# Attention scores of the second block: q's high part stacked over k's high and low parts, in one-pass matmuls

## The reference

```python
def chunked_rel_attention(q, k, v, rel_bias):
    ...
    s = jnp.einsum('bcqhd,bckhd->bhcqk', qc, kb).astype(jnp.float32) * (hd ** -0.5) + bias[None, :, None]
    ...
    s = jnp.where(valid[None, None, :, None, :], s, jnp.finfo(jnp.float32).min)
    p = jax.nn.softmax(s, axis=-1).astype(v.dtype)
    o = jnp.einsum('bhcqk,bckhd->bcqhd', p, vb)

def hybrid_mixer(x, mix_norm, w_in, ...):
    h = rms_norm(x, mix_norm)
    proj = h @ w_in
    ...
    xbc = jax.nn.silu(causal_depthwise_conv(xbc, conv_w, conv_b))
    y = ssd_chunked(xs, dt, a, bm, cm, d_skip).reshape(bsz, seqlen, SSD_INNER)
    y = rms_norm(y * jax.nn.silu(z.astype(jnp.float32)), ssd_norm).astype(x.dtype)
    att = chunked_rel_attention(...)
    return jnp.concatenate([y, att], axis=-1) @ w_out
```

## Time and profile before

| | |
|---|---|
| three runs, median (lowest to highest) | 2024.4 us (2022.7 to 2024.58) |
| the profiled execution, its own time | 2024.56 us |
| its span in the trace | 2022.8 us |
| PE busy | 1943.0 us, 96% |
| DVE, ACT, POOL busy | 972.6, 837.1, 791.6 us |
| the loop over the pairs | about 1344 to 1579 us, one pair 59.7 us |
| records of the score matmuls (line 814) | 64, 25.7 us busy |

### The profile page before, as it was taken

How to read it: one execution, slowest core, us unless ns; L and a number is a source line. 1 busy time by engine, 2 the same in 40 slices (tenths; PEclk the granted TensorE clock), 3 DMA queues, 4 the chain that set the end, 5 groups by cost and what they waited for, 6 DMA issues and landing times.

```text
span 2022.8 us, 25020 instructions
## 1 busy us (share of the span) xinstructions
PE 1943.0 (96%) x8654; PEld 1559.7 (77%) x8654; DVE 972.6 (48%) x1099; ACT 837.1 (41%) x1072; POOL 791.6 (39%) x353
## 2 busy tenths in 40 slices
PE   2999999998999999999999999999998999999998
PEld 1777777776788888888888888777676788888886
DVE  6666666666534333223344331447786634344323
ACT  2566666663455554223232222355555323232221
POOL 4222222224344444444444444432222344444443
PEclk9999999999899999999999999899999999999999
DMA  6233333331222222222222233222111222222321
GB/s 274 103 126 124 124 123 126 124 125 69 75 94 97 95 94 102 94 102 85 99 98 93 95 104 107 79 84 73 67 68 54 73 93 94 97 100 93 104 104 73
DMA packets 54324, 202.59 MB, mean 100 GB/s; under 512 B 6032, under 2 KB 6160, under 8 KB 53392
## 3 DMA queue, kind: packets, MB, share of 16 engines
q1 hardware_dynamic: 54288, 202.10, 28.3%
HBM read 199.98 MB, written 2.10 MB: 100 GB/s over the span
## 4 chain that ended last, share of the span: by engine, by line
PE 90%; DVE 5%; issue 1%; ACT 1%; POOL 1%; DMA 1%; DVEq 0%; SPq 0%; ACTq 0%; POOLq 0%
PE bank L543 26%; PE bank L548 26%; PE bank L544 26%; PE bank L909 1%; PE bank L910 1%; PE bank L911 1%; PE bank L654 1%; PE bank L628 1%; PE bank L663 1%; POOL SS L448 1%; DVE MIX L1571 1%; DVE SQ L1573 1%; DMA XT<-in_xt 1%; PE bank L814 1%; DVE MIX L1246 1%
## 5 line engine op out<-in xcount | busy, mean ns | idle before, releaser
L456 POOL TENSOR_TENSOR WL<-ring,WH 128x1024 fp32r<-128x1024 f32 x309 | 755.2, 2444 | 1164.3 <-ACT WH L934 1164.2
L543 PE MATMUL bank<-HH,WL 128*128 128x512 f32 x1864 | 744.8, 400 | 9.8 <-ACT HH L955 4.4
L544 PE MATMUL bank<-HH,WH 128*128 128x512 f32 x1864 | 731.4, 392 | 0.0
L934 ACT ACTIVATE WH<-ring 128x1024 fp32r<-128x1024 f32 x317 | 335.5, 1060 | 935.7 <-PE bank L548 865.9
L548 PE MATMUL bank<-HL,WH 128*128 128x512 f32 x1864 | 464.1, 391 | 0.9 <-DVE HL L1246 0.8
L543 PEld LDWEIGHTS bank<-HH,WL 128*128 128x128 f32 x1864 | 353.3, 190 | 92.9 <-issue 13.6
L544 PEld LDWEIGHTS bank<-HH,WH 128*128 128x128 f32 x1864 | 353.4, 190 | 76.1 <-issue 4.3
L548 PEld LDWEIGHTS bank<-HL,WH 128*128 128x128 f32 x1864 | 351.1, 188 | 76.0 <-DVE HL L1246 3.2
L544 PE MATMUL bank<-FH,WH 128*128 128x512 f32 x544 | 211.8, 389 | 0.0
L543 PE MATMUL bank<-FH,WL 128*128 128x512 f32 x544 | 211.7, 389 | 0.0
L548 PE MATMUL bank<-FL,WH 128*128 128x512 f32 x544 | 135.0, 389 | 0.0
(11 more groups left out here) (266 smaller groups left out, 1825.6 us busy)
## 6 DMA issues: line engine op xcount, KB each, us to landing
ring<-in_stream SPq DMA_DIRECT2D x365, 512.0 KB, 3.2
ARENA<-in_ada SPq DMA_DIRECT2D x6, 1024.0 KB, 18.3
XT<-in_xt SPq DMA_DIRECT2D x1, 2048.0 KB, 12.2
result<-XT SPq DMA_DIRECT2D x4, 512.0 KB, 2.7
vec<-in_vec SPq DMA_DIRECT2D x1, 220.0 KB, 2.5
```

What stands on the lines that cost most here:

```text
L456: nc.gpsimd.tensor_tensor(WL[:, slot, :], ring[:, u % RING, :], WH[:, slot, :].bitcast(F32), ALU.subtract).then_inc(w_low, 1)
L543: mm(out_ap, part(WL, base, loc, k), xh(k), start=(start and k == 0), stop=False)
L544: mm(out_ap, part(WH, base, loc, k), xh(k), start=False, stop=False)
L934: A(WH[:, split_at(base, loc)[1], :], ring[:, u % RING, :], ACT.Copy).then_inc(w_high, 1)
```

## The change

q and k are kept as fp32r high and low parts, stacked in 128 partitions. Per head of a pair: QA holds q's high part twice (rows of both halves), KA holds k's high part in one half and its low part in the other, QB holds q's low part in the half where KA has k's high part and zeros in the other. A segment of scores is then two fp32r matmuls over 128 rows, QA by KA and QB by KA, in place of one fp32 matmul over 64 rows. ACT copies q four times and k twice, each 64 partitions by 512, in place of one copy of 128 partitions each. DVE gets `k_low` (two instructions behind distance x2), `q_low` of the next pair (two, behind taps(0)) and ahead of the loop two zero fills and the first `q_low`. The waits on qk_evac become waits on q_high, q_low, k_high and k_low.

```diff
+        with ExitStack() as stacks:
+            STACKS = stacks.enter_context(nc.sbuf_tensor("STACKS", [P, 6 * S], F32R))
...
-                        first = mm(bank[b][:, c:c + w], N["Q2"][hh * 64:(hh + 1) * 64, i * P:(i + 1) * P],
-                                   N["K2"][hh * 64:(hh + 1) * 64, 0:w], start=(i != 0), stop=False, skip_group_check=True)
+                        first = mm(bank[b][:, c:c + w], N[f"QA{hh}"][:, i * P:(i + 1) * P], N[f"KA{hh}"][:, 0:w],
+                                   start=(i != 0), stop=False, skip_group_check=True)
+                        mm(bank[b][:, c:c + w], N[f"QB{hh}"][:, i * P:(i + 1) * P], N[f"KA{hh}"][:, 0:w],
+                           start=False, stop=False, skip_group_check=True)
...
-                pe.wait_ge(r["qk_evac"], 2 * t + 1)
+                pe.wait_ge(r["q_high"], 4 * t + 4)
+                pe.wait_ge(r["q_low"], 2 * t + 4)
...
-                pe.wait_ge(r["qk_evac"], 2 * t + 2)
+                pe.wait_ge(r["k_high"], 2 * t + 2)
+                pe.wait_ge(r["k_low"], 2 * t + 2)
                 scores(0)
...
-                A(N["Q2"], bank[4][:, :], ACT.Copy, scale=0.125).then_inc(r["qk_evac"], 1)
+                for to in (0, 1):
+                    for hh in (0, 1):
+                        half = slice(64 * (hh ^ to), 64 * (hh ^ to) + 64)
+                        A(N[f"QA{hh}"][half, :], bank[4][64 * hh:64 * (hh + 1), :], ACT.Copy, scale=0.125).then_inc(r["q_high"], 1)
...
-                A(N["K2"], bank[6][:, :], ACT.Copy).then_inc(r["qk_evac"], 1)
+                for hh in (0, 1):
+                    half = slice(64 * hh, 64 * (hh + 1))
+                    A(N[f"KA{hh}"][half, :], bank[6][half, :], ACT.Copy).then_inc(r["k_high"], 1)
...
+            def q_low(t):
+                dve.wait_ge(r["q_high"], 4 * t + 4)
+                for hh in range(2):
+                    half = slice(64 * hh, 64 * (hh + 1))
+                    STT(N[f"QB{hh}"][half, :], bank[4][half, :], 0.125, N[f"QA{hh}"][half, :].bitcast(F32),
+                        ALU.mult, ALU.subtract).then_inc(r["q_low"], 1)
+
+            def k_low(t):
+                dve.wait_ge(r["k_high"], 2 * t + 2)
+                for hh in range(2):
+                    half, other = slice(64 * hh, 64 * (hh + 1)), slice(64 * (1 - hh), 64 * (2 - hh))
+                    TT(N[f"KA{hh}"][other, :], bank[6][half, :], N[f"KA{hh}"][half, :].bitcast(F32),
+                       ALU.subtract).then_inc(r["k_low"], 1)
+
+            for hh in range(2):
+                half = slice(64 * (1 - hh), 64 * (2 - hh))
+                V.tensor_copy(N[f"QB{hh}"][half, :], zero[half, 0:1].to_broadcast([64, S])).then_inc(r["q_low"], 1)
+            q_low(0)
...
                 distance(0, 1, 4)
+                k_low(t)
                 select(1, 0, t)
...
                     taps(0, 3, t + 1)
+                    q_low(t + 1)
```

More of the change, by code:

```diff
@@ L229, in mixer2_tiles @@
             d["CT"] = t(2 * S)
+            d["Q2"] = t(S)
+            d["K2"] = t(S)
             d["GS"] = t(2 * TRI)
@@ L238, in mixer2_tiles @@
             d["PT1"] = t(TRI)
-            d["Q2"] = t(S)
-            d["K2"] = t(S)
             d["V2"] = t(S)
@@ L254, in mixer2_tiles @@
             d["BC"] = d["ED0"][:, 0:S]
+            for at, n in enumerate(("QA0", "QA1", "KA0", "KA1", "QB0", "QB1")):
+                d[n] = tile_of(STACKS, at)
             d["XS"] = [CG[:, 0, :], CG[:, 1, :]]
@@ L349, in program @@
                  "g_mm g_evac g_mask xs_conv xs_tap xs_silu xs_tr xd_done sel_done csb_done "
-                 "dd_done ed_done mm_done y_mm y_skip z_silu yz_done yss_done qk_evac v_evac v_tr pv_mm "
+                 "dd_done ed_done mm_done y_mm y_skip z_silu yz_done yss_done q_high q_low k_high k_low v_evac v_tr pv_mm "
                  "s_mm s_add s_max s_neg s_exp s_rec s_nrm t_mm t_evac o_high o_low "
```

## The result

| | before | after |
|---|---|---|
| median of 20 runs each (lowest to highest) | 2024.76 us (2022.7 to 2026.98) | 2028.91 us (2026.98 to 2030.69) |
| span of the profiled execution | 2022.8 us | 2028.5 us |
| PE busy | 1943.0 us | 1935.5 us |

The ratio is 1.0019, with 1.0013 to 1.0026 as its 95% interval. The changed kernel is **slower by 4.1 us**. The forecast was 2033.3 us, in the range of 2019 to 2042; its sign was right, its size twice too large (+8.7 us). A second series of 11 runs gave 2028.69 us.

The account below looks back on a forecast made before the run. PE was taken as the bound, nine tenths of the chain that ended last. First halves -7.2, collisions +7.2 and clock falls +8.7 gave +8.7 us on 2024.56: 2033.3 us, range 2019 to 2042.

Parts of the forecast that it names:

- Scores and the first half: Up to turn(0): scores blocks last 1.6 us instead of 3.46, k_low mostly fits DVE's idle time; 4 x -1.8 = -7.2 us.
- The trigger: Before turn(1): earlier PE lets ACT write unit 11 at once, so POOL has its next unit ready when unit 10 ends.
- The collision: At normalise(1): POOL's unit 11 gets in after DVE's first instruction, delaying turn(1); 3 x +2.4 = +7.2 us.
- The clock: After PE's 5.5 us waits before turn(1): half clock for 4.7 to 7.5 us; 3 x +2.9 = +8.7 us.
- A: At normalise(1): DVE's lined-up instructions are not parted by POOL; 2017.4 us, or 2026.1 if the clock falls; chance 0.16.
- C: In the scores: new matmuls save little, 1 us a head, and the second half still collides; +11.9, 2036.5 us; chance 0.05.
- D: Before turn(1): the wait grows but the clock stays up at 5.5 us; change 0, 2024.6 us; chance 0.07.
- B: In the first half: times_g's second instruction is held by POOL's unit 6; +0.5 us a pair, 2040.2 us; chance 0.17.

Follow-up runs that it names:

- the hold: Changed kernel with one more ACT wait: the high part of unit 11 is written only when normalise(1) is done; 2017.95 us, ratio 0.9968.
- the padding: Changed kernel with 8 matmuls of 512 columns, result thrown away, ahead of projection 8 in the first three pairs; 2017.76 us, ratio 0.9965.
- the kernel before with PE early: Kernel before the change, with the two widest fp32 matmuls of each pair's second scores block replaced by one-pass ones on constants; 2037.82 us, ratio 1.0064.
- the nudge: Changed kernel with an unread DVE copy of 128 columns ahead of times_g(0, 0) in each pair; 2036.96 us, ratio 1.0061.

## Why the prediction was right in sign and twice too large

**Scores and the first half: right.** 1.62 us for a block where 1.6 was forecast. That the sum fits is in part luck: by the distances between starts the eight matmuls take 1.47 us and not 1.17, the four masks 0.15 and not 0.4. The half gains 1.67 us on average and not 1.8: k_low costs 0.28 us of the 1.92 that PE gives (run without k_low). q's four copies and q_low were costed at nothing, and the rests of 15.01 to 15.03 us in the pairs without a clock fall, as before the change, show it. ACT's four copies, 2.42 us, ended in time.

**The trigger: right.** That a faster PE lets ACT write unit 11 at once, and that POOL then splits two units in a row through normalise(1), is shown by the hold and by the padding, which take it away by different means, and by the kernel before with PE early, which brings it about alone.

**The collision: right, a little too dear.** +2.11 a pair for +2.4. I let the first instruction stand behind POOL's first split and three behind the second. In the trace the first gets through between the splits, and the second is stuck but has begun. POOL is busy for 4.64 us in place of 2.39, 2.25 more, and what DVE still has to do behind POOL's end takes 0.88 us in place of 1.08 (1456.54 to 1457.42; before, 1453.13 to 1454.21). So normalise(1) grew by 2.05 us; the last 0.06 us came ahead of it.

The Trainium skill (SBUF — State Buffer, "Who interferes with whom") gives the shared ports to whoever issues first, for the whole instruction. The trace agrees with it instruction by instruction: POOL's second split began 0.05 us ahead of DVE's second. What I set against it in the prediction, the handover of the earlier trace rows, is the same rule applied to each instruction and not to the four as a group.

**The clock: the mechanism right, the size wrong.** This is the step that failed, the third sum, 3 x +2.9 = +8.7 us. The clock did fall in all three waits of 5.2 us. I took 4.7 to 7.5 us of half clock after PE went on from the two stretches of the earlier trace rows. It was 6.0, 4.5 and 3.8 us in the first profile, and the rests grew by 2.80, 2.06 and 1.73 us. There are fifteen such falls in the profiles of the changed kernel (twice), of the kernel before with PE early, of the one without k_low and of the nudge. Half clock lasted 3.3 to 6.0 us after PE went on, 4.4 on average, and the rests grew by 1.6 to 2.8 us, 2.0 on average. For the changed kernel the term is thus +6.6 and +5.5 us in its two profiles and +4.5 to +4.85 by the medians against the run that kept PE busy. The price of a us of half clock was right: I charged 0.48, and it was 0.46. The length was wrong. I had two stretches, both behind other kinds of work, and took their lengths for that of any fall; the low end I allowed, 2.2, lies above the average.

In thirteen of the fifteen the clock had fallen while PE still waited, and what passed of it with PE idle cost nothing. That does not explain the short lengths, for in the run without k_low the clock stayed up through two of the waits and fell only when PE had gone on. The rows are such a wait and the stretch behind it, in its second pair:

```profile
1449.00:1454.10 5.10, 0.00 (x0) 0.00 (x0) 5.10 (x5) 1.14 (x2) 4.26 (x2) 1.00 0.45 159
1454.40:1457.70 3.30, 3.30 (x14) 3.01 (x14) 1.89 (x3) 1.15 (x3) 0.00 (x0) 0.50 0.47 158
```

The two rests grew by 1.6 us, among the least of the fifteen. What sets the length stays open: it differs among three pairs that run the same instructions.

**The sum.** -6.7 + 6.3 and three falls at 1.6 to 2.0 give +4.4 to +5.6; with the last row of the first table (-0.8 to -0.9) it is +3.6 to +4.7, against +4.15 measured. That last row I had as zero. It is the clock again: behind the last turn(1) PE ran the same instructions at half clock for 5.8 us before the change and for 4.3 us after it.

```profile
1571.40:1577.20 5.80, 5.80 (x19) 3.06 (x20) 2.27 (x4) 1.62 (x4) 0.00 (x0) 0.50 0.06 24
1577.30:1578.50 1.20, 1.20 (x14) 0.60 (x10) 0.00 (x0) 0.00 (x0) 0.00 (x0) 1.00 0.00 0
...
1577.10:1581.40 4.30, 4.30 (x15) 2.74 (x16) 1.11 (x3) 1.62 (x4) 0.00 (x0) 0.50 0.02 7
1581.50:1583.50 2.00, 2.00 (x16) 0.84 (x12) 1.06 (x2) 0.00 (x0) 0.00 (x0) 1.00 0.00 0
```

Over all the profiles this stretch takes 6.14 to 7.26 us. The kernel before with PE early, which has nothing of the change, takes 6.25, so the -0.8 is not shown to come from the change.

**Rivals.** A (DVE's instructions are not parted) fell: normalise(1) takes 5.46 us. C fell: a head saves 1.84 us. D fell: PEclk 0.50. **B did not happen, by 0.01 us:** in the first three pairs the second times_g began 0.011, 0.011 and 0.015 us ahead of POOL's split, kept the ports and made POOL take 3.75 us. The nudge shows what lay on the other side: +2.33 us a first half in place of B's +2.3 (0.5 and not -1.8), and a time of 2036.96 where B had 2040.2, lower by the too large clock term that it shared. To know which side it would be, one needed times to 0.02 us ahead of the change, and the prediction could place that instruction only to 0.2 us.

On what favoured B, the Trainium skill (VectorE: DVE Perf Modes, "Two Vector instructions with no wait between them") has an instruction held whose operands start in another quadrant of partitions. Here the two of k_low, 0.69 us each, took 1.41 together and so did not overlap, where two of times_g, 1.49 each, took 2.89: the trace agrees.

## What to carry to other kernels

Before taking time from the engine that bounds, ask whose work it releases earlier, and lay that beside the steps the engine will wait for next: here 1.9 us less on PE set off 2.1 us of port collisions and up to 2.8 us of half clock, and one wait on ACT, which cost nothing here, made the same change worth 6.5 us of gain. Where a gain vanishes, make the fast engine slow again at that place by dummy work: if the kernel gets faster, the loss hangs on when that engine arrives, and an order of work may cure it. A margin of hundredths of a microsecond between a DVE and a POOL instruction in a loop is worth finding and widening, since here either side of it differed by 8 us.

## What was unexpected of the hardware

- A clock fall of the same cause costs different amounts from pair to pair: 1.6 to 2.8 us after waits of about 5 us, and 1.26 us after one wait of 3.1 us. Of the three such waits in that run the clock fell in one; the wait of 3.2 us in the earlier trace rows had left it alone.
- Width is no protection against the shared ports: a DVE instruction on 4 columns was stuck for 2.04 us behind a POOL split.
- A bf16 mask matmul of 128 columns holds PE 0.04 us up to the next start where a one-pass matmul comes next, and 0.16 where an fp32 one does. So three masks a block got cheaper, by 0.36 us together; the fourth stood ahead of a one-pass product before the change too, and held PE 0.04 us (the row below this list, to 1419.51). About 0.19 us of the 0.36 comes back in the one-pass matmul behind a mask: with 384 columns it takes 0.26 us up to the next start, and the one behind it, of the same width, 0.17.
- An instruction on 64 partitions is not cheaper than one on 128. On DVE it is 0.69 us for 512 columns in both; ACT's copies of q take 0.6 us each (four in 2.42), and the one copy of 128 partitions before the change took 0.58.

```profile
1419.47 0.23 PE L818 MATMUL bank<-chunkb,identb 128*128 128x128 bf16 x1
```
